# The inverse of a long convolution in split operands, with the output weights fetched behind its first half

## The reference, cut to what matters

```python
def hyena_mixer(u, w_in, b_in, conv_w, conv_b, f_w1, ..., decay, skip, w_out, b_out):
    L = u.shape[1]                                   # 512
    z = short_conv(u @ w_in + b_in, conv_w, conv_b)
    x0, x1, v = jnp.split(z, 3, axis=-1)
    s = (v * x1).astype(jnp.float32)
    g = hyena_filter(L, f_w1, ..., decay)            # (2L, D), two-sided
    n = 2 * L
    y = jnp.fft.irfft(jnp.fft.rfft(s, n=n, axis=1) * jnp.fft.rfft(g, n=n, axis=0)[None],
                      n=n, axis=1)[:, :L]            # the inverse that the change touches
    y = (y + s * skip.astype(jnp.float32)).astype(u.dtype) * x0
    return y @ w_out + b_out                         # hy_out
```

## Time and profile before

| | |
|---|---|
| median of 3 runs | 1371.04 us |
| the profiled execution's own time | 1370.73 us |
| its span, first to last instruction | 1368.9 us |
| TensorE busy | 1357.0 us, 99% |
| VectorE busy | 949.1 us, 69% |
| ScalarE busy | 607.7 us, 44% |
| GpSimd busy | 122.1 us, 9% |
| forward, from the first `forward_s` matmul to the inverse | 910.1 to 937.5 us |
| inverse, up to the first `hy_out` matmul | 937.5 to 966.1 us |

### The profile page before, as it was taken

The page is one execution under the profiler, slowest core; times in us unless marked ns, Lnnn a source line. Parts: engine busy times, 40 slices in busy tenths (PEclk is TensorE's granted clock), DMA queues, the critical chain, the costliest instruction groups (busy, mean ns, idle before and its releaser), DMA issues.

```text
span 1368.9 us, 18308 instructions
## 1 busy us (share of the span) xinstructions
PE 1357.0 (99%) x6944; PEld 1134.3 (83%) x6944; DVE 949.1 (69%) x1302; ACT 607.7 (44%) x842; POOL 122.1 (9%) x143
## 2 busy tenths in 40 slices
PE   9999999999999999999999999999999999999997
PEld 7777886888788888888888888878888899989986
DVE  7767788555666755763676786777878689548944
ACT  6546686333444533431344554443344445325532
POOL 1010156000000000000000221014000000000000
PEclk9999999999999999999999999999999999999999
DMA  7222345421122332222321332341222332322321
GB/s 274 98 97 78 123 153 187 154 92 62 62 76 81 121 123 92 92 92 101 112 95 61 104 112 92 108 144 57 92 93 96 110 133 93 119 97 93 105 81 62
DMA packets 28160, 144.40 MB, mean 105 GB/s; under 512 B 3211, under 2 KB 8612, under 8 KB 13497
## 3 DMA queue, kind: packets, MB, share of 16 engines
q1 hardware_dynamic: 24744, 133.97, 28.7%
q0 software_dynamic: 2656, 8.72, 1.8%
q10 hardware_dynamic: 688, 0.73, 0.2%
HBM read 136.84 MB, written 6.30 MB: 105 GB/s over the span
## 4 chain that ended last, share of the span: by engine, by line
PE 94%; DVE 2%; ACT 1%; DMA 1%; issue 1%; SPq 0%; POOL 0%; DVEq 0%; ACTq 0%
PE ps L2127 28%; PE ps L2129 28%; PE ps L2128 28%; PE ps L2543 1%; PE ps L2345 1%; PE ps L2358 1%; PE ps L2493 1%; PE ps L2335 1%; PE ps L2384 1%; PE ps L2679 1%; PE ps L2681 1%; PE ps L2685 1%; PE ps L2386 0%; PE ps L2385 0%; DMA h<-x_t_dram 0%
## 5 line engine op out<-in xcount | busy, mean ns | idle before, releaser
L2127 PE MATMUL ps<-opA_hi,w_hi 128*128 128x512 f32 (+1 forms) x1008 | 385.0, 382 | 0.8 <-DVE w_lo L1302 0.4
L2129 PE MATMUL ps<-opA_hi,w_lo 128*128 128x512 f32 (+1 forms) x1008 | 380.9, 378 | 0.0
L2128 PE MATMUL ps<-opA_lo,w_hi 128*128 128x512 f32 (+1 forms) x1008 | 380.5, 378 | 0.0
L1302 DVE TENSOR_TENSOR w_lo<-raw,w_hi 128x2048 fp32r<-128x2048 f32 x112 | 256.6, 2291 | 87.1 <-ACT w_hi L727 85.7
L727 ACT CAST w_hi<-raw 128x2048 fp32r<-128x2048 f32 x111 | 211.6, 1907 | 233.2 <-PE ps L2129 232.9
L2127 PE MATMUL ps<-opB_hi,w_hi 128*128 128x512 f32 (+1 forms) x584 | 226.8, 388 | 1.7 <-DVE opB_lo L1338 1.0
L2129 PE MATMUL ps<-opB_hi,w_lo 128*128 128x512 f32 (+1 forms) x584 | 225.6, 386 | 0.0
L2128 PE MATMUL ps<-opB_lo,w_hi 128*128 128x512 f32 (+1 forms) x584 | 225.6, 386 | 0.0
L2127 PEld LDWEIGHTS ps<-opA_hi,w_hi 128*128 128x128 f32 x1008 | 189.8, 188 | 37.4 <-issue 1.9
L2129 PEld LDWEIGHTS ps<-opA_hi,w_lo 128*128 128x128 f32 x1008 | 189.7, 188 | 35.6
L2128 PEld LDWEIGHTS ps<-opA_lo,w_hi 128*128 128x128 f32 x1008 | 189.8, 188 | 34.0 <-issue 0.2
(11 more groups left out here) (452 smaller groups left out, 2027.9 us busy)
## 6 DMA issues: line engine op xcount, KB each, us to landing
raw<-weights_dram SPq DMA_DIRECT2D x113, 1024.0 KB, 4.9
g_dram<-g_stage POOLq DMA_DIRECT2D x8, 512.0 KB, 3.0
h<-x_t_dram SPq DMA_DIRECT2D x7, 512.0 KB, 7.2
g_spec<-g_dram SPq DMA_DIRECT2D x5, 512.0 KB, 3.4
scores<-g_dram SPq DMA_DIRECT2D x3, 512.0 KB, 4.9
out_dram<-h SPq DMA_DIRECT2D x6, 256.0 KB, 2.3
mem_raw<-mem_t_dram POOLq DMA_DIRECT2D x1, 1024.0 KB, 8.3
c_keys<-c_dram POOLq DMA_DIRECT2D x4, 256.0 KB, 3.7
```

The lines of the kernel that those rows point to most:

```text
L1302: V.tensor_tensor(w_lo[:, p, :], raw[:, p, :], w_hi[:, p, :].bitcast(F32), ALU.subtract).then_inc(lo_ready, 1)
L2127: W.matmul(out, w[0], x[0], start=start, stop=False, skip_group_check=mixed)
L2128: W.matmul(out, w[0], x[1], start=False, stop=False, skip_group_check=mixed)
L2129: return W.matmul(out, w[1], x[0], start=False, stop=stop, skip_group_check=mixed)
```

## The change

- The inverse matrices and the filtered spectrum are split. The four blocks of `inv` are laid out anew, each padded to an even number of columns, with zeros where the padding comes; ScalarE patches those (`inv_patch`, four operations), makes `inv_hi` (1540 columns) and `inv_hi_es` (512), VectorE makes `inv_lo` in place of `inv`.
- The spectrum's high parts `y_hi` are made by ScalarE (`spectrum_hi(half, q)`, 128x1024 each, eight of them), the low parts `y_lo` by VectorE (`spectrum_lo`, eight), in place of `y_spec`. `y_hi` of half 0 lies in `raw`, that of half 1 in `spec`; `inv_hi` lies in slot 1 of `w_hi`, `inv_lo` in slot 1 of `w_lo`.
- Each product of the inverse is now `passes`, three fp32r matmuls of 256 or 258 columns. TensorE waits for `y_lo` where it waited for `spec_sum`, and for `pair_ready(I_PAIR)`, the low part of the matrices.
- Both Nyquist rows are copied by ScalarE out of the split spectrum.
- SP fetches both `hy_out` pairs after `inv_done` 4, when half 0 of the inverse is done, and no longer before. ScalarE casts pair 0 behind `hyena_out_hi(4)`, and pair 1 behind `even_part(7)`, once `inv_done` is 8. VectorE's two weight subtractions move back as well.

The core of the diff:

```diff
-EC, OS, ES, OC = 0, 2 * (HALF + 1), 2 * (HALF + 1) + T, 4 * HALF + T
+EC, OS, OC, ES = 0, T + 4, 2 * T + 4, 3 * T + 4
+INV_COLS = 4 * T + 4
...
-        inv = at("inv", [P, 2 * CHUNK], F32, 120 * KB)
+        inv, inv_lo = at("inv", [P, INV_COLS], F32, 120 * KB), at("inv_lo", [P, INV_COLS], F32R, 120 * KB)
+        inv_hi = at("inv_hi", [P, ES], F32R, 104 * KB)
...
+        y_lo = [at("y_lo0", [P, KT, T], F32R, 16 * KB), at("y_lo1", [P, KT, T], F32R, 32 * KB)]
...
+        y_hi = [at("y_hi0", [P, KT, T], F32R, 80 * KB), at("y_hi1", [P, KT, T], F32R, c1 + 50 * KB)]
...
-            sp.wait_ge(lo_ready, F_PAIR)
-            sp.dma_start(raw[:, 1, :], a["weights"][in_dram(I_PAIR + 2)]).then_inc(raw_in[1], 16)
...
-            sp.wait_ge(lo_ready, F_PAIR + 1)
-            sp.dma_start(raw[:, 0, :], a["weights"][in_dram(I_PAIR + 1)]).then_inc(raw_in[0], 16)
...
             for n in range(3, 8):
                 sp.wait_ge(fs_read, n - 2)
                 load_spectrum(n)
+            sp.wait_ge(inv_done, 4)
+            for p in range(2):
+                sp.dma_start(raw[:, p, :], a["weights"][in_dram(I_PAIR + 1 + p)]).then_inc(raw_in[p], 16)
...
-                             used={F_PAIR: (fs_done, 8), I_PAIR: (chunk_done, 2 * F_PAIR)}.get(g))
+                             used={F_PAIR: (fs_done, 8), I_PAIR: (inv_done, 8)}.get(g))
...
+            def inv_split_hi():
+                act.wait_ge(inv_patched, 4)
+                A.copy(inv_hi[:], inv[:, 0:ES]).then_inc(inv_patched, 1)
+                act.wait_ge(nyq_row_made, 2)
+                A.copy(inv_hi_es[:], inv[:, ES:]).then_inc(hi_ready, 1)
+
+            def spectrum_hi(half, q):
+                act.wait_ge(spec_sum, 8 * half + 2 * q + 2)
+                if q == 0:
+                    act.wait_ge(row_zero, 2 * half + 2)
+                A.copy(y_hi[half][:, 2 * q:2 * q + 2, :], y_spec[half][:, 2 * q:2 * q + 2, :]).then_inc(y_hi_made, 1)
...
-            nyquist_hi(0)
-            nyquist_hi(1)
-            split_after(F_PAIR)
-            split_after(I_PAIR)
-            for c in range(KT):
+            nyquist_rows(0)
+            act.wait_ge(spec_sum, 14)
+            spectrum_hi(1, 0)
+            spectrum_hi(1, 1)
+            even_part(0)
+            act.wait_ge(spec_sum, 16)
+            spectrum_hi(1, 2)
+            spectrum_hi(1, 3)
+            nyquist_rows(1)
+            even_part(1)
+            hyena_out_hi(0)
+            for c in range(2, KT):
                 even_part(c)
-                if c:
-                    hyena_out_hi(c - 1)
+                if c == KT - 1:
+                    split_after(I_PAIR)
+                hyena_out_hi(c - 1)
+                if c == 5:
+                    split_after(F_PAIR)
...
             for n in range(8):
-                if n == 7:
-                    nyquist_lo(0)
                 spectrum_products(n)
-            nyquist_lo(1)
+                if 2 <= n < 6:
+                    spectrum_lo(0, n - 2)
+                if n == 3:
+                    dve.wait_ge(hi_ready, I_PAIR + 1)
+                    S.link(lo_part(inv_lo[:, 0:ES], inv[:, 0:ES], inv_hi[:]))
+                    lo_part(inv_lo[:, ES:], inv[:, ES:], inv_hi_es[:]).then_inc(lo_ready, 1)
+            spectrum_lo(1, 0)
+            spectrum_lo(1, 1)
             V.engine_nop().then_inc(bank_read, 4)
             for c in range(KT):
-                if c == 4:
+                hyena_value(c)
+                if c == 0:
+                    spectrum_lo(1, 2)
+                    spectrum_lo(1, 3)
+                    continue
+                if c == KT - 1:
+                    split_after(I_PAIR)
+                hyena_out_lo(c - 1)
+                if c == 6:
                     split_after(F_PAIR)
-                hyena_value(c)
-                if c:
-                    hyena_out_lo(c - 1)
-                if c == 6:
-                    dve.wait_ge(inv_done, 8)
-                    split_after(I_PAIR)
...
+                        if q < 2:
+                            last = passes(bank[:, HALF - 2:T], y_re, columns(EC + q * (HALF + 2), HALF + 2), q == 0, False, mixed=True)
...
+                            passes(bank[:, 0:HALF], y_im, columns(ES + q * HALF, HALF, back=True), False, False, mixed=True)
                         else:
...
+                            passes(bank[:, 0:HALF], y_re, columns(OC + (q - 2) * HALF, HALF, back=True), False, False, mixed=True)
+                            passes(bank[:, HALF:T], y_im, columns(OS + (q - 2) * HALF, HALF), False, False, mixed=True)
...
-            pe.wait_ge(inv_patched, 1)
-            pe.wait_ge(hi_ready, I_PAIR + 1)
+            pair_ready(I_PAIR)
```

More of the change, by code:

```diff
@@ L145, in program @@
         acc = at("acc", [P, T], F32, o)
-        nyq_row = at("nyq_row", [1, HALF + 1], F32, o); o += 2048
+        nyq_row = at("nyq_row", [1, HALF + 1], F32, o)
+        inv_hi_es = at("inv_hi_es", [P, T], F32R, o); o += 2048
         sq_at = o
@@ L353, in program @@
         BY_8, T_BASE, HI_BASE = 8, 16, 24
+        y_hi_made, y_lo_made, Y_LO_BASE = y_nyq_hi, fwd_patched, 4
         block = ctx.enter_context(nc.Block())
@@ L1184, in hyena_out_hi, with nyquist_rows @@
                 A.copy(op_hi[1][:, c, :], hy_val_feat[:, c % 4, :]).then_inc(u_hi, 1)
-            def nyquist_hi(half):
+            def nyquist_rows(half):
                 act.wait_ge(nyq_cleared, 8 + half)
-                act.wait_ge(row_zero, 2 * half + 2)
-                A.copy(y_nyq[half][0:1, :], y_spec[half][0:1, 1, :]).then_inc(y_nyq_hi, 1)
+                act.wait_ge(y_hi_made, 4 * half + 1)
+                A.copy(y_nyq[half][0:1, :], y_hi[half][0:1, 1, :]).then_inc(y_nyq_lo, 1)
+                act.wait_ge(y_lo_made, Y_LO_BASE + 4 * half + 1)
+                A.copy(y_nyq[half][32:33, :], y_lo[half][0:1, 1, :]).then_inc(y_nyq_lo, 1)
             row_zero_products(0)
+            act.wait_ge(lo_ready, F_PAIR + 1)
+            spectrum_hi(0, 0)
             inv_patch()
@@ L1947, in hyena_out_lo, with spectrum_lo @@
                 lo_part(op_lo[1][:, c, :], hy_val_feat[:, c % 4, :], op_hi[1][:, c, :]).then_inc(u_lo, 1)
[L1950 to L1953, removed]
+            def spectrum_lo(half, q):
+                dve.wait_ge(y_hi_made, 4 * half + q + 1)
+                tiles = slice(2 * q, 2 * q + 2)
+                lo_part(y_lo[half][:, tiles, :], y_spec[half][:, tiles, :], y_hi[half][:, tiles, :]).then_inc(y_lo_made, 1)
             for n in range(8):
-                if n == 7:
-                    nyquist_lo(0)
                 spectrum_products(n)
-            nyquist_lo(1)
+                if 2 <= n < 6:
[6 more added lines that the diff above has]
+            spectrum_lo(1, 1)
             V.engine_nop().then_inc(bank_read, 4)
             for c in range(KT):
-                if c == 4:
-                    split_after(F_PAIR)
-                hyena_value(c)
-                if c:
-                    hyena_out_lo(c - 1)
-                if c == 6:
-                    dve.wait_ge(inv_done, 8)
-                    split_after(I_PAIR)
+                hyena_value(c)
[7 more added lines that the diff above has]
+                if c == 6:
+                    split_after(F_PAIR)
             hyena_out_lo(KT - 1)
@@ L2653, in inverse, with columns @@
             def inverse(half):
-                y = y_spec[half]
+                def columns(start, count, back=False):
+                    if back:
+                        own = slice(start - ES + count - 1, start - ES - 1 if start > ES else None, -1)
+                        whole = slice(start + count - 1, start - 1, -1)
+                        return (inv_hi_es[:, own] if start >= ES else inv_hi[:, whole]), inv_lo[:, whole]
+                    return inv_hi[:, start:start + count], inv_lo[:, start:start + count]
                 for c in range(4):
-                    cs = slice(c * P, (c + 1) * P)
                     bank = ps[:, 4 + c, :]
@@ L2662, in inverse @@
                         if c == 0:
[L2663 to L2676, removed]
-                        else:
[L2678 to L2686, removed]
+                            pe.wait_ge(y_lo_made, Y_LO_BASE + 4 * half + q + 1)
+                        y_re, y_im = ([part[half][:, 2 * q + f, c * P:(c + 1) * P] for part in (y_hi, y_lo)] for f in range(2))
+                        if q < 2:
+                            last = passes(bank[:, HALF - 2:T], y_re, columns(EC + q * (HALF + 2), HALF + 2), q == 0, False, mixed=True)
+                            if half and c == 0 and q == 0:
+                                last.then_inc(chunk_done, 4)
+                            passes(bank[:, 0:HALF], y_im, columns(ES + q * HALF, HALF, back=True), False, False, mixed=True)
+                        else:
+                            passes(bank[:, 0:HALF], y_re, columns(OC + (q - 2) * HALF, HALF, back=True), False, False, mixed=True)
```

(5 more changed lines are left out.)

16 lines of the change are left out of this document (12 added, 4 removed).

## The result

The changed kernel takes 1383.07 us (median of 4 runs, 1382.52 to 1385.16) against 1370.99 us for the kernel before beside it (4 runs, 1370.71 to 1371.67): 1.0092 times the time of before, 95% interval 1.0080 to 1.0104, 12.1 us slower. Its profiled execution took 1383.3 us, with a span of 1381.5 us.

A forecast was written before the change was run, and what follows sets the result against it. TensorE was taken to bound the kernel, with VectorE close behind in the inverse. A 9.8 us wait plus 2.4 us of clock loss gave 12.2 on 1370.73, forecast 1383.2 us, range 1376.0 to 1386.5.

The forecast's parts named there:

- TensorE's saving: Inverse on TensorE: split passes of 0.12 us, 3.0 us per tile, 24.0 us in all, a gain of 4.6 us.
- Backward streaming: Rival in the inverse: backward-streamed passes take 0.24 us, 4.4 us per tile; +11.3, 1382.3 us; chance 0.08.
- VectorE's walk: VectorE's queue from the third spectrum product, step by step in its new order, to the first output weights' low part at 975.8.
- The turns: At the matrices and second-half `y_lo`, VectorE and GpSimd alternate whole operations: 2 x 1.25 us, then 0.5 and 1.2.
- Without turns: Rival: GpSimd and VectorE collide less; `hy_out` at 971.1, +5.0, with the clock +7.4, 1378.4 us; chance 0.20.
- The wait before `hy_out`: TensorE stands 10 us for the first output weights' low part; `hy_out` starts at 975.9 against 966.10, +9.8 us.
- That later inverse: TensorE's inverse was walked to start at 941.9, take 12.0 us per half and be done at 965.9.
- the stand before n = 6: TensorE waits 4 us for spectrum product 4, until 935.6; a possible clock cost there has 10 us of slack behind it.
- The clock's return: After the idle stand `hy_out` starts at 1.2 GHz; half of a 4.8 us return is lost, +2.4 us.
- The rival without a clock loss: In `hy_out` the clock costs nothing; only +9.8 remains, 1380.8 us; chance 0.14.
- The second pair: Second `hy_out` weight pair ready at 980.4, while TensorE's tiles before it last until 981.5: no second wait.
- Slack at the weight load: Weights in SBUF by about 965, ScalarE's cast at 967.6: hidden, 4 us to spare until VectorE asks at 973.6.

The follow-up runs named there:

- e5: The changed kernel with GpSimd's 16 sums of the spectrum replaced by constant fills, so the sums are left out; 1377.27 us, ratio 1.0044.
- e3: The changed kernel with 70 matmuls more on TensorE, results unused, between the inverse and `hy_out`; 1380.93 us, ratio 1.0075.
- e2: The changed kernel with only the first `hy_out` weight pair's cast and subtraction earlier, the second pair left as changed; 1382.35 us, ratio 1.0087.
- e1_both_early: The changed kernel with both `hy_out` weight pairs' casts and subtractions earlier in their queues, the fetch as changed; 1373.89 us, ratio 1.0025.
- e6_early_inv_later: e1_both_early with the two `inv_lo` subtractions moved from behind spectrum product 3 to behind product 5; 1374.25 us, ratio 1.0028.
- e4: The kernel before, whole-operand inverse kept, with only the late fetch and late splits of the `hy_out` weights; 1374.11 us, ratio 1.0026.

## Why the prediction was right, point by point

- **TensorE's saving.** 0.12 us a pass and 2.96 us a tile, as walked. The inverse shrank by 4.9 us, not 4.6. Backward streaming costs nothing extra (0.12 us), so that rival is out.
- **VectorE's walk.** Each of its five marks came within 0.4 us. The walk has 1.7 us of wait for GpSimd's last sums and `y_hi` (945.1 to 946.8); it was 1.3 (945.3 to 946.58).
- **The turns.** Assumed: 2.5 us at the matrices and 1.7 in the second half. Measured against e5: 2.1 and 1.6. Without turns the walk had promised 4.8 us less, 0.6 more than these two terms, which the prediction doesn't account for. e5 gave 5.8, and 1.2 of it is the wait for `y_hi`: the fills are also shorter than the sums, so e5 bounds the turns from above.
- **The wait before `hy_out`.** Predicted start 975.9, measured 975.63: +9.5 for +9.8. The stand is 9.0 us, not 10, since the inverse began 0.8 us later than walked (942.7 for 941.9) and ended at 966.4 for 965.9.
- **That later inverse** is a step that was mis-sized: the stand before n = 6 also halved the clock (it reads 0.50 from 938 to 940 us), which I held possible but did not put into the walk. At half clock forward n = 6 took so long that n = 7, walked to wait until 939.1, had no wait at all. The stand before `hy_out` hid the delay, as said.
- **The clock's return.** Predicted 2.4, measured 2.8 by the rows and 2.1 by e3's medians (1.6 to 2.8 by all the comparisons above). The rival without a clock loss is out.
- **The second pair** was no second wait. Its low part was ready at 980.1 (977.92 + 2.2; predicted 980.4), and TensorE, at half rate, came to it only at about 983.9 (predicted 981.5). e2 shows what stands there when the first wait is mended alone: 7.0 us.
- **Slack at the weight load.** ScalarE's cast came at 967.28 (967.6 predicted), 4 us ahead of VectorE; the fetch was hidden.

The sum of 12.2 met 12.1 measured, with terms off by 0.3 and 0.4 us the opposite way; that they cancel is luck. It rests on the queue's order being fixed in the code: each term was a count times a duration from this engine at this shape.

## What to carry to other kernels

A faster TensorE stage gains nothing when the engine beside it is nearly full in that stage and gets the extra work: walk the neighbour's queue in its new order, with every new operation at its measured distance, before counting the saving. An operation that a later stage waits for should stand in the queue by when it is needed, not where its data's new fetch suggests; mend such waits together, since the next stands right behind (0.7 us for one, 9 for both). A stand of TensorE can also cost its clock's return (2 to 3 us here); and what depends on the shape alone need not be split on the chip.

## What was not expected of the hardware

Nearly the same stand before forward n = 6 was followed by half clock in one kernel and not in another. In the kernel after it lasts 3.33 us, and the windows show the clock falling only after TensorE had resumed at 935.50:

```profile
934.00:936.00 2.00, 0.50 (x2) 0.46 (x3) 2.00 (x4) 0.00 (x0) 0.47 (x1) 1.00 0.00 0
936.00:938.00 2.00, 2.00 (x8) 1.58 (x8) 2.00 (x4) 0.00 (x0) 2.00 (x2) 0.74 0.75 227
938.00:940.00 2.00, 2.00 (x7) 1.51 (x6) 2.00 (x3) 1.00 (x2) 1.92 (x2) 0.50 0.09 35
940.00:942.00 2.00, 2.00 (x9) 1.63 (x8) 1.83 (x4) 0.14 (x1) 2.00 (x2) 0.91 0.00 0
```

In e1_both_early it lasts 3.31 us:

```profile
934.85 0.50 PE L2169 MATMUL ps<-opB_hi,w_hi 128*128 128x512 f32 x1 [3.31 <-DVE spec L1964]
```

and the clock stays at full:

```profile
936.00:938.00 2.00, 1.90 (x9) 1.21 (x7) 2.00 (x4) 0.00 (x0) 2.00 (x2) 1.00 0.61 231
938.00:940.00 2.00, 1.62 (x7) 1.35 (x8) 1.82 (x3) 1.14 (x2) 1.93 (x2) 1.00 0.00 0
```

In e6_early_inv_later a shorter stand, ahead of the inverse, was followed by half clock, and the inverse took 25.3 us there in place of 23.7:

```profile
940.11 0.58 PE L2169 MATMUL ps<-inv_hi,y_hi 128*128 128x258 f32 x1 [2.55 <-DVE inv_lo L1373]
```

```profile
940.00:942.00 2.00, 1.89 (x9) 1.89 (x10) 2.00 (x5) 1.24 (x2) 0.00 (x0) 0.52 0.03 8
```

So the length of a stand alone doesn't decide here: 2.55 and 3.33 us were followed by half clock, 3.31 and e4's 2.40 were not. Each is one profiled execution, so whether it is chance or the kernel is open. The return times differ as well: from the first matmul to full rate it took 5.7 us after the stand of 9 us, 4.9 after the one of 3.33 (935.50 to 940.40), 3.4 in e6 (940.11 to 943.49), and 4.8 at the start of the kernel by the counts of the earlier trace rows.
